# Short convolution: projections of chunks 1 to 3 as wide products in bank pairs, their sums kept in SBUF

## What is computed

```python
def _causal_dwconv(x, w):
    """Causal depthwise conv over positions. x: (B,S,C), w: (K,C); y[t] = sum_k w[k] x[t-K+1+k]."""

def _short_conv_mixer(x, w_in, conv_w, w_out):
    """LFM2-style: y = W_out(B * conv3(C * h)), [B, C, h] = W_in x."""
    b_gate, c_gate, h = jnp.split(x @ w_in, 3, axis=-1)
    return (b_gate * _causal_dwconv(c_gate * h, conv_w)) @ w_out

# first_block, i = 0
y = _short_conv_mixer(x, sc_w_in[j], sc_conv_w[j], sc_w_out[j])
x = _layer_norm(ALPHA * x + y, ln_mix_g[i], ln_mix_b[i])
x = _layer_norm(ALPHA * x + _sq_relu_mlp(x, ff_w1[i], ff_w2[i]), ln_ff_g[i], ln_ff_b[i])
```

## Time and profile before

| | |
|---|---|
| median of three runs | 1098.77 us (1098.38 to 1100.83) |
| profiled execution | 1098.84 us, its span 1097.0 us |
| PE busy | 1074.2 us, 98% of the span |
| DVE busy | 694.9 us, 63% |
| ACT busy | 536.7 us, 49% |
| mean DMA rate | 184 GB/s |
| short convolution | about 10 to 101 us of the span |

### The profile page before, as it was taken

The page is one execution under the profiler, slowest core; times in us unless marked ns, Lnnn a source line. Parts: engine busy times, 40 slices in busy tenths (PEclk is TensorE's granted clock), DMA queues, the critical chain, the costliest instruction groups (busy, mean ns, idle before and its releaser), DMA issues.

```text
span 1097.0 us, 15412 instructions
## 1 busy us (share of the span) xinstructions
PE 1074.2 (98%) x6149; PEld 942.8 (86%) x6149; DVE 694.9 (63%) x771; ACT 536.7 (49%) x629; POOL 51.2 (5%) x99
## 2 busy tenths in 40 slices
PE   8999999999999999999989999999999999999997
PEld 7998888888988888888868888888999888888886
DVE  4767756565675766565666555554888766555562
ACT  5543544444366354444445444445756646444442
POOL 1000000000200100000010000002030100000000
PEclk9999999999999999999989999999999999999999
DMA  9864766654571585655536656654785355656631
GB/s 315 281 225 153 237 191 191 191 192 137 157 245 59 169 240 188 193 189 191 192 131 221 193 184 191 193 156 115 203 240 189 116 192 172 202 186 191 195 109 38
DMA packets 141025, 201.71 MB, mean 184 GB/s; under 512 B 9144, under 2 KB 116896, under 8 KB 140976
## 3 DMA queue, kind: packets, MB, share of 16 engines
q1 hardware_dynamic: 138048, 191.25, 55.1%
q0 software_dynamic: 2928, 9.79, 2.7%
HBM read 199.95 MB, written 1.06 MB: 183 GB/s over the span
## 4 chain that ended last, share of the span: by engine, by line
PE 96%; DVE 2%; ACT 1%; issue 1%; POOL 0%; DVEq 0%; POOLq 0%; ACTq 0%
PE up L1693 23%; PE acc L1704 12%; PE acc L1705 12%; PE acc L1707 12%; PE up L1696 12%; PE up L1644 4%; PE up L1646 4%; PE up L1645 4%; PE acc L1818 2%; PE acc L1826 2%; PE acc L1819 2%; PE up L1759 1%; PE up L2010 1%; PE acc L2151 1%; ACT x_parts L619 1%; PE up L1670 1%
## 5 line engine op out<-in xcount | busy, mean ns | idle before, releaser
L1099 DVE TENSOR_TENSOR weight_lo<-raw,weight_hi 128x2048 fp32r<-128x2048 f32 (+4 forms) x184 | 411.3, 2239 | 121.4 <-ACT weight_hi L619 121.0
L619 ACT ACTIVATE weight_hi<-raw 128x2048 fp32r<-128x2048 f32 (+4 forms) x184 | 343.1, 1869 | 139.3 <-PE acc L1707 127.1
L1693 PE MATMUL up<-x_parts,weight_hi 128*128 128x512 f32 x1088 | 271.5, 391 | 0.0
L1693 PEld LDWEIGHTS up<-x_parts,weight_hi 128*128 128x128 f32 x1088 | 198.5, 188 | 37.5
L1704 PE MATMUL acc<-weight_hi,hh 128*128 128x512 f32 x480 | 187.5, 391 | 0.9 <-issue 0.9
L1705 PE MATMUL acc<-weight_lo,hh 128*128 128x512 f32 x480 | 187.4, 390 | 0.0
L1696 PEld LDWEIGHTS up<-x_parts,weight_lo 128*128 128x128 f32 x1088 | 148.4, 190 | 10.6
L1696 PE MATMUL up<-x_parts,weight_lo 128*128 128x256 f32 x1088 | 151.7, 282 | 0.0
L1707 PE MATMUL acc<-weight_hi,hl 128*128 128x512 f32 x480 | 151.3, 389 | 0.0
L1707 PEld LDWEIGHTS acc<-weight_hi,hl 128*128 128x128 f32 x480 | 90.1, 188 | 19.1
L1704 PEld LDWEIGHTS acc<-weight_hi,hh 128*128 128x128 f32 x480 | 90.3, 188 | 18.5 <-issue 1.5
(11 more groups left out here) (244 smaller groups left out, 1057.5 us busy)
## 6 DMA issues: line engine op xcount, KB each, us to landing
raw<-in_ff_w SPq DMA_DIRECT2D x64, 1024.0 KB, 5.5
raw<-in_ffn_w_down SPq DMA_DIRECT2D x22, 1024.0 KB, 5.0
raw<-in_ffn_w_gate SPq DMA_DIRECT2D x20, 1024.0 KB, 5.4
raw<-in_ffn_w_up SPq DMA_DIRECT2D x20, 1024.0 KB, 5.4
raw<-in_w_in SPq DMA_DIRECT2D x14, 1024.0 KB, 6.0
raw<-in_sc_w_in SPq DMA_DIRECT2D x11, 1024.0 KB, 9.0
raw<-in_w_out SPq DMA_DIRECT2D x6, 1024.0 KB, 6.0
raw<-in_sc_w_out SPq DMA_DIRECT2D x4, 1024.0 KB, 6.0
```

The lines of the kernel that those rows point to most:

```text
L619: return nc.scalar.activation(dst, src, ACT.Copy, **kw)
L1099: return vec.tensor_tensor(dst, whole, high.bitcast(F32), ALU.subtract)
L1693: mm(bank.rearrange("p (a n) -> p a n", a=2), w_h[k], x_parts[:, k, :, :], start=k == 0, stop=k == KD - 1, skip_group_check=True)
```

## The change

In chunks 1 to 3 the projections are made by `wide_product`. Part p of chunk c (slab number u = 3(c-1) + p, counted from slab 3) goes to bank pair 0,1 if u is even, to pair 2,3 if odd. For each slab ACT now copies the small part to SBUF (`part_out`), and DVE adds the main part to it (`part_sum`). B's sum and h's sum lie in a part of `arena` that is unused in this stage (`b_sum`, two buffers, and `h_sum`), C's in `tmp_a`. In chunk 0 the product stays as it was, but ACT copies B to `b_sum[0]` as well. All these copies count in one semaphore, `copied`, the sums in `summed`. PE waits before slab u for the sum of slab u-2, which empties the bank pair; at slab 3 it waits for three copies, at slab 4 for chunk 0's C * h.

```diff
@@ -205,6 +205,8 @@
         g_kv = take(KV_LORA)
         prob_a = take(2 * 384, 2, 384)
         v_a = normed
+        b_sum = (arena[:, 0:HALF], arena[:, HALF:2 * HALF])
+        h_sum = arena[:, 2 * HALF:3 * HALF]
         latent_q = normed[:, 0, 0:2 * Q_LORA].rearrange("p (t n) -> p t n", t=TILES)
         latent_kv = normed[:, 1, 0:2 * KV_LORA].rearrange("p (t n) -> p t n", t=TILES)
 
@@ -244,7 +246,7 @@
         landed = [sem(f"landed{i}") for i in range(RING)]
         hi_done, lo_done, slab_used = sem("hi_done"), sem("lo_done"), sem("slab_used")
         act_step, dve_step, pool_step = sem("act_step"), sem("dve_step"), sem("pool_step")
-        cols_turned, cols_ready, pool_ready = sem("cols_turned"), sem("cols_ready"), sem("pool_ready")
+        cols_turned, pool_ready = sem("cols_turned"), sem("pool_ready")
 
         class Sems:
 
@@ -261,7 +263,7 @@
         turned, operand_high, operand_low, acc_part, seeded = (
             sem("turned"), sem("operand_high"), sem("operand_low"), sem("acc_part"), sem("seeded"))
         fresh = Sems("fresh", "sum act hidden turned hi")
-        sc = Sems("sc", "c_copied ch_made conv0 y_made y_hi chunk")
+        sc = Sems("sc", "copied summed ch_made conv0 y_made y_hi chunk")
         mlp = Sems("mlp", "small_out summed squared hidden_hi chunk")
         glu = Sems("glu", "small_out summed gate hidden hidden_hi chunk")
         mla = Sems("mla", "rows latent_ps sumsq rstd latent turned t_hi t_lo pe q_out swapped rotated k_ps k_out v0 v1")
@@ -691,39 +693,54 @@
             for m in range(1, RING):
                 round_slab(m)
 
+            def part_out(dst, b):
+
+                copy(pair(dst[:, :]), small_part(b)).then_inc(sc["copied"], 1)
+
             m = S_SC
             for c in range(SC_CHUNKS):
                 if c == 0:
                     act.wait_ge(cols_turned, 1)
-                    copy(cols[:, :], up[3][:, 0:ROWS]).then_inc(cols_ready, 1)
-                    act.wait_ge(cols_ready, 1)
-                if c < SC_CHUNKS:
-                    round_slab(m + RING)
-                    act.wait_ge(slab_used, m + 2)
-                    if c == 1:
-                        for n in range(2 * TILES):
-                            seed(n, (x_landed[n // 2], 16), ALPHA)
-                    if c:
-                        act.wait_ge(sc["ch_made"], c)
-                    copy(tmp_a[:, :], up[1][:, :]).then_inc(sc["c_copied"], 1)
-                    round_slab(m + 1 + RING)
-                    act.wait_ge(sc["ch_made"], c + 1)
-                    if c:
-                        act.wait_ge(sc["y_made"], c)
-                    for f in range(CT):
-                        tap = cols[:, ROW_SC + (SC_TAPS - 1) * KD + CT * c + f:][:, 0:1]
-                        nc.scalar.activation(tmp_c[:, f * TOKENS:(f + 1) * TOKENS],
-                                             tmp_b[:, f * TOKENS:(f + 1) * TOKENS], ACT.Copy, scale=tap)\
-                            .then_inc(sc["conv0"], 1)
+                    copy(cols[:, :], up[3][:, 0:ROWS]).then_inc(sc["copied"], 1)
+                    copy(b_sum[0], up[0][:, :]).then_inc(sc["copied"], 1)
+                else:
+                    act.wait_ge(slab_used, m + 1)
                     if c >= 2:
-                        round_slab(m + 2 + RING)
-                        act.wait_ge(slab_used, DOWN[c - 2] + 1)
-                    act.wait_ge(sc["y_made"], c + 1)
-                    copy(hh[:, CT * (c % 2):CT * (c % 2) + CT, :],
-                         tmp_d[:, :].rearrange("p (f n) -> p f n", f=CT)).then_inc(sc["y_hi"], 1)
-                    if c < 2:
-                        round_slab(m + 2 + RING)
-                    m += 3
+                        act.wait_ge(sc["y_made"], c - 1)
+                    part_out(b_sum[c % 2], 2 * ((c - 1) % 2))
+                round_slab(m + RING)
+                act.wait_ge(slab_used, m + 2)
+                if c == 1:
+                    for n in range(2 * TILES):
+                        seed(n, (x_landed[n // 2], 16), ALPHA)
+                if c:
+                    act.wait_ge(sc["ch_made"], c)
+                    part_out(tmp_a, 2 * (c % 2))
+                else:
+                    copy(tmp_a[:, :], up[1][:, :]).then_inc(sc["copied"], 1)
+                round_slab(m + 1 + RING)
+                if c:
+                    act.wait_ge(slab_used, m + 3)
+                    part_out(h_sum, 2 * ((c - 1) % 2))
+                act.wait_ge(sc["ch_made"], c + 1)
+                if c == 0:
+                    act.wait_ge(sc["copied"], 1)
+                else:
+                    act.wait_ge(sc["y_made"], c)
+                for f in range(CT):
+                    tap = cols[:, ROW_SC + (SC_TAPS - 1) * KD + CT * c + f:][:, 0:1]
+                    nc.scalar.activation(tmp_c[:, f * TOKENS:(f + 1) * TOKENS],
+                                         tmp_b[:, f * TOKENS:(f + 1) * TOKENS], ACT.Copy, scale=tap)\
+                        .then_inc(sc["conv0"], 1)
+                if c >= 2:
+                    round_slab(m + 2 + RING)
+                    act.wait_ge(slab_used, DOWN[c - 2] + 1)
+                act.wait_ge(sc["y_made"], c + 1)
+                copy(hh[:, CT * (c % 2):CT * (c % 2) + CT, :],
+                     tmp_d[:, :].rearrange("p (f n) -> p f n", f=CT)).then_inc(sc["y_hi"], 1)
+                if c < 2:
+                    round_slab(m + 2 + RING)
+                m += 3
                 if c == 2:
                     round_slab(m + RING)
                     m += 1
@@ -1193,15 +1210,28 @@
                 split_slab(m)
 
 
+            def part_sum(c, part, t):
+
+                dve.wait_ge(sc["copied"], 3 * c + part + 1)
+                vec.tensor_tensor(pair(t[:, :]), main_part(2 * ((c - 1 + part) % 2)), pair(t[:, :]), ALU.add)\
+                    .then_inc(sc["summed"], 1)
+
             m = S_SC
             for c in range(SC_CHUNKS):
+                if c:
+                    part_sum(c, 0, b_sum[c % 2])
                 split_slab(m + RING)
+                if c:
+                    part_sum(c, 1, tmp_a)
                 split_slab(m + 1 + RING)
-                dve.wait_ge(slab_used, m + 3)
-                dve.wait_ge(sc["c_copied"], c + 1)
-                vec.tensor_tensor(tmp_b[:, :], up[2][:, :], tmp_a[:, :], ALU.mult).then_inc(sc["ch_made"], 1)
-                if c == 0:
-                    dve.wait_ge(cols_ready, 1)
+                if c:
+                    part_sum(c, 2, h_sum)
+                    dve.wait_ge(sc["summed"], 3 * c)
+                    vec.tensor_tensor(tmp_b[:, :], h_sum, tmp_a[:, :], ALU.mult).then_inc(sc["ch_made"], 1)
+                else:
+                    dve.wait_ge(slab_used, m + 3)
+                    dve.wait_ge(sc["copied"], 3)
+                    vec.tensor_tensor(tmp_b[:, :], up[2][:, :], tmp_a[:, :], ALU.mult).then_inc(sc["ch_made"], 1)
                 dve.wait_ge(sc["conv0"], CT * (c + 1))
                 for back in (1, 2):
                     for f in range(CT):
@@ -1211,8 +1241,7 @@
                             tmp_c[:, o + back:o + TOKENS], tmp_b[:, o:o + TOKENS - back], cols[:, row:row + 1],
                             tmp_c[:, o + back:o + TOKENS], ALU.mult, ALU.add)
                     then(ins)
-                b_bank = up[3 if c % 2 else 0]
-                vec.tensor_tensor(tmp_d[:, :], b_bank[:, :], tmp_c[:, :], ALU.mult).then_inc(sc["y_made"], 1)
+                vec.tensor_tensor(tmp_d[:, :], b_sum[c % 2], tmp_c[:, :], ALU.mult).then_inc(sc["y_made"], 1)
                 if c >= 2:
                     split_slab(m + 2 + RING)
                 dve.wait_ge(sc["y_hi"], c + 1)
@@ -1769,8 +1798,6 @@
 
             m = S_SC
             for c in range(SC_CHUNKS):
-                if c == 1:
-                    pe.wait_ge(cols_ready, 1)
                 if c == 0:
                     first_product(m, up[0])
                     first_product(m + 1, up[1])
@@ -1778,16 +1805,16 @@
                     nc.tensor.transpose(up[3][:, 0:ROWS], rows[:, :], ident[0:ROWS, 0:ROWS]).then_inc(cols_turned, 1)
                     first_product(m + 2, up[2])
                 else:
-                    weights(m)
-                    if c >= 2:
-                        pe.wait_ge(sc["y_made"], c - 1)
-                    up_product(m, up[3 if c % 2 else 0])
-                    weights(m + 1)
-                    pe.wait_ge(sc["c_copied"], c)
-                    up_product(m + 1, up[1])
-                    weights(m + 2)
-                    pe.wait_ge(sc["ch_made"], c)
-                    up_product(m + 2, up[2])
+                    for part in range(3):
+                        used = 3 * (c - 1) + part
+                        weights(m + part)
+                        if used == 0:
+                            pe.wait_ge(sc["copied"], 3)
+                        elif used == 1:
+                            pe.wait_ge(sc["ch_made"], 1)
+                        else:
```

(2 more changed lines are left out.)

## The result

The changed kernel takes 1101.68 us (median of 12 runs, 1100.59 to 1104.38), the kernel before 1099.09 us (12 runs, 1098.20 to 1100.83). The ratio is 1.0027, with a 95% interval of 1.0019 to 1.0035: slower by 0.27%. The forecast was 1101.2 us, in a range of 1099.5 to 1104.0.

What follows compares the result with a forecast made beforehand. PE bounds the kernel, busy 1074.2 of 1097.0 us, so new waits are lost in full. Waits of 0.15 + 3.2 + 0.15 + 0.5 = 4.0 us less 1.6 saved, on 1098.84, give 1101.2 us; range 1099.5 to 1104.0.

Steps and rivals of the forecast that it cites:

- The pace: Wide products of slabs 3 to 11 and 12 on PE: 5.58 us each instead of 5.76, nine slabs saving 1.6 us.
- The cost of the copies and sums: Seven ACT copies (4.1 us in all) and nine DVE sums (6.2 us): the work costs nothing, only its place counts.
- Slab 3: PE waits there for three copies, the last that of C ending at 27.53 us: 0.15 us lost.
- Slab 5: PE waits there for slab 3's sum, behind `hh`, rounding and copy on ACT and slab 6's split on DVE: 3.2 us.
- Slab 8: PE waits there for slab 6's sum, behind chunk 1's `hh`, rounding and slab 9's split: 0.15 us lost, 0 to 0.4.
- the last products: Their second slab waits for chunk 3's `hl`, delayed by a copy and a sum: 0.5 us lost, 0.2 to 0.8.
- The clock: Rival: PE's clock falls to 1.2 GHz in slab 5's wait, costing 2.1 us more, 1103.3 us in all; chance 0.27.
- The argument against: Against a clock fall at slab 5: matmuls stand close on both sides, with no shorter wait just ahead.
- the long wait: PE's idle time before slab 5, waiting for slab 3's sum: 3.2 us, with ends 3.0 to 3.4.
- the rival's 1103.3: Total in us if the clock falls in slab 5's wait, up to 1104.5 if it came back late; chance 0.27.
- Not slower with a short wait at slab 5: Rival: slab 3's sum comes soon after slab 4, wait at most 0.8 us: 1098.8 us, 1098.0 with none; chance 0.10.
- That a later stage gives nothing back: After the short convolution everything hangs on PE, so all behind it is shifted by some 2.4 us.

Runs made afterwards that it cites:

- experiment 4: Changed kernel with the B sums of chunks 1 and 2 made early and slab 12 made by the narrow product again: 1097.82 us, ratio 0.9987 to the kernel before.
- experiment 8: Changed kernel with B sums of chunks 1 and 2 early, slab 12 narrow, and waits near 553 and 556 us filled with zero matmuls: 1095.32 us, ratio 0.9970.
- experiment 5: Kernel before, with PE's waits near 553 and 556 us filled with matmuls of zeros (7 and 14): 1096.77 us, ratio 0.9983.
- experiment 6: Changed kernel with only the later waits near 556 us filled with matmuls of zeros, slab 5's wait left empty: 1100.28 us, ratio 1.0008.
- experiment 1: Changed kernel with chunk 1's B copied before chunk 0's `hh` and summed before its `hl`: 1100.00 us, ratio 1.0006 to the kernel before.
- experiment 3: Kernel before, with one line making PE wait at slab 5 for the split of slab 6: 1100.99 us, ratio 1.0013.
- experiment 10: Changed kernel with only chunk 1's B sum early, and the later waits near 556 us filled with zero matmuls: 1097.89 us, ratio 0.9991.
- experiment 9: Changed kernel with B sums of chunks 1 and 2 early, all nine products wide, and the later waits filled: 1095.63 us, ratio 0.9968.
- experiment 7: Changed kernel with zero matmuls filling both the wait at slab 5 and those near 556 us: 1099.22 us, ratio 1.0006 to the kernel before.

## Why the prediction was right, step by step

*The pace.* 5.58 us for a wide slab was forecast, 5.59 measured. That the time falls by a saving of this size is shown by experiment 4 (1.4 us for eight slabs) and by experiment 8 against 5 (1.45 us).

*The cost of the copies and sums* was forecast as nothing but their place. Experiments 4 and 8 keep nearly all of them (ACT makes one copy and DVE one sum less) and gain what the wide products save. Right.

*Slab 3* was to lose 0.15 us and lost nothing: C's copy ended at 26.98 us (26.40 and 0.58), before slab 3 began at 27.20. In this execution the rounding of slab 4, behind which it stands, came 0.5 us earlier, released by its load.

*Slab 5* was to be 3.2 us late and was 3.1, by the forecast order of `hh`, rounding, copy, split and sum. In experiment 6 it was a little less, 2.7 us of idle time and 0.16. *Slab 8* was to lose 0.15 and lost 0.1; *the last products* 0.5 and lost 0.5.

*The clock* is where I gave the wrong weight. I held it likelier that it stays (0.53) than that it falls (0.27), and my likeliest time contains no fall. By the two groups of experiment 6 and their mean clocks it fell in seven executions of eleven, and the groups differ by 1100.3 - 1098.7 = 1.6 us (I had said 2.1, from one case). In the profiled execution of the changed kernel it took 2.9 us. The argument against, that matmuls stand close on both sides, doesn't hold: experiments 1 and 3 show the fall behind waits of 1.91 and 2.00 us with dense work on both sides. But the fall isn't certain there: in the profile of experiment 10 the clock held through a wait of 1.96 us. What decides between the two is open. The Trainium skill (TensorE: Matmul & The Clock Gate, section "HAM oscillation — how this bites in real kernels") describes pauses of about 3 to 5 us between bursts that throw the array back to the half clock each time. These profiles agree in kind and differ in size: here waits of 1.91 to 2.93 us did it, and not in every execution.

So the sum without a fall is 1098.62 to 1098.81 (experiment 6) against 1096.77 (experiment 5), 1.9 us, where I had 2.4. The 0.15 at slab 3 and 0.3 of the long wait make the difference. The fall adds to it in a part of the executions, and the median of 1101.68 us lies between the forecast 1101.2 and the rival's 1103.3, nearer to the forecast. That it came so near is partly luck. The terms without a fall were 0.5 us too high, and a fall in seven of eleven executions adds 1.0 us on average that the sum doesn't have. The means of the result's runs differ by 1102.1 - 1099.1 = 3.0 us, those of experiments 6 and 5 by 1099.8 - 1096.9 = 2.9, as 1.9 and 1.0 give; the forecast had 2.4.

Two small slips in the working change nothing: the chances given for slower add up to 0.72, not 0.71, and the upper ends of the terms to 1102.1 us, not 1102.0.

*Not slower with a short wait at slab 5* was the rival on the other side. Its condition was right but not enough: experiment 1 fulfils it and takes 1100.0 us, not 1098.0, because the wait moves to slab 8. Only with that sum early too (experiments 4 and 9) is the gain there.

*That a later stage gives nothing back* is shown by the profiles. The changed kernel is 4.9 us later both at 118 us and at 560 us (564.52 against 559.62). And without a fall the terms at slab 5, at slab 8 and in the last products less the saving, 2.85 + 0.1 + 0.5 - 1.5, give the 1.9 us between experiments 5 and 6.

## What to carry to other kernels

When a product now needs its result added from two parts before a bank is free, the copy and the sum are short, but each stands in an engine's program behind longer work; put them where the bank's next user needs them, and after removing one wait work out the next again, since a late engine hides what comes after. On the engine that bounds the kernel every new wait is lost in full: here 1.5 us saved in nine pieces were more than lost at one semaphore. Where a wait of PE like these (1.9 to 3.4 us) can't be removed, a few matmuls of zeros into a free bank can keep its clock; near 556 us this was worth 2.15 us with two calls, at slab 5 about 1 us (experiment 7 against 6).

## What the runs showed of the hardware

The granted clock fell in waits of PE of 1.91, 2.00, 2.69 and 2.93 us that had dense matmuls on both sides (profiles of experiments 1, 3 and 6 and of the changed kernel), and held in one of 1.96 us (profile of experiment 10). By the groups of times it fell in seven executions of eleven at a wait of 2.7 us (experiment 6) and in at most three or four of twelve at one of 2.0 us (experiment 10). In a wait of 1.83 us ahead of the first product it fell in the profile of experiment 8 and held in those of both kernels. The loss was 1.6 us by the groups of experiment 6 and up to 2.9 us in one profile. I had not expected it in waits this short.

The wait of 3.44 us near 556 us, which the kernel always had, cost 2.15 us by the clock alone (1098.92 against 1096.77, with the shorter wait of 1.94 us just ahead filled too), and filling it also took most of the spread out of the times: 1097.88 to 1100.64 before, ten of eleven runs in 1096.23 to 1096.94 with the fill.

A matmul of this number format pays 13 to 15 ns beside its columns (0.120 us from start to start for 256 columns, 5.47 / 24 = 0.228 us for 512, against 0.107 and 0.213 us at 2.4 GHz). Nine slabs with 144 matmuls fewer for the same columns took 9 x 0.17 = 1.5 us less.
